# Two transformer blocks on one core: softmax scaling taken from the probabilities and put on the attention output

## What is computed

```python
# first block: kinds "a" (top-k selected keys, biased) and "b" (latent attention)
logits = jnp.where(mask, logits, -jnp.inf)
p = jax.nn.softmax(logits, axis=-1)
y = jnp.einsum('bhts,bshd->bthd', p, v)

# second block: kind "A" (mixture of dilated windows) and three branches with gates
def masked_softmax(logits, mask):
    p = jnp.exp(logits - m)
    den = jnp.sum(p, axis=-1, keepdims=True)
    return p / jnp.maximum(den, 1e-30)
gate = jax.nn.sigmoid(gl)
o_b = gate[..., 0:1] * o_cmp + gate[..., 1:2] * o_slc + gate[..., 2:3] * o_win
```

## Time and profile before

| | |
|---|---|
| median of 3 runs | 2970.11 us (2968.42 to 2970.17) |
| the profiled execution's own time | 2971.57 us |
| its span | 2969.6 us |
| busy PE / DVE / ACT / POOL | 88% / 50% / 22% / 68% |
| attention of block one, two layers | 338 to 454 and 1382 to 1499 us |
| attention of block two | 2335 to 2513 us |

### The profile page before, as it was taken

How to read it: one execution, slowest core, us unless ns; L and a number is a source line. 1 busy time by engine, 2 the same in 40 slices (tenths; PEclk the granted TensorE clock), 3 DMA queues, 4 the chain that set the end, 5 groups by cost and what they waited for, 6 DMA issues and landing times. The chain is left out here.

```text
span 2969.6 us, 35964 instructions
## 1 busy us (share of the span) xinstructions
PE 2617.5 (88%) x11363; PEld 1905.5 (64%) x11363; DVE 1480.9 (50%) x2231; ACT 647.6 (22%) x1406; POOL 2017.7 (68%) x988
## 2 busy tenths in 40 slices
PE   6876788989999988857889889999889888899998
PEld 3652456767777756524567667777587655677776
DVE  4789644336715437896353367244520243443243
ACT  1312451013201113124520123011100365110001
POOL 4562467877878865624568778788668744688886
PEclk9996888999999989977889999999869888899999
DMA  5130001222322222300012222222443100233232
GB/s 152 57 100 22 22 1 59 90 78 78 92 85 86 91 72 64 100 22 22 1 56 89 83 71 92 85 92 85 113 128 122 49 1 8 65 95 96 92 92 78
DMA packets 62115, 214.33 MB, mean 72 GB/s; under 512 B 6384, under 2 KB 6512, under 8 KB 61984
## 3 DMA queue, kind: packets, MB, share of 16 engines
q1 hardware_dynamic: 54144, 195.06, 21.2%
q10 hardware_dynamic: 7840, 17.58, 2.2%
HBM read 210.45 MB, written 10.01 MB: 74 GB/s over the span
## 5 line engine op out<-in xcount | busy, mean ns | idle before, releaser
L398 PE MATMUL out_tile<-arena_r,w_hi 128*128 128x512 f32 (+1 forms) x5474 | 1760.1, 403 | 0.0
L1388 POOL TENSOR_TENSOR w_hi<-weight_ring,cst 128x1024 fp32r<-128x1024 f32 x363 | 891.1, 2455 | 713.1 <-issue 508.5
L398 PE MATMUL out_tile<-arena_r,w_lo 128*128 128x512 f32 (+1 forms) x2737 | 1144.7, 418 | 126.5 <-DVE arena_r L1050 67.0
L398 PEld LDWEIGHTS out_tile<-arena_r,w_hi 128*128 128x128 f32 (+1 forms) x5474 | 1058.0, 194 | 249.7 <-issue 9.9
L1392 POOL TENSOR_TENSOR w_lo<-weight_ring,w_hi 128x1024 fp32r<-128x1024 f32 x363 | 903.4, 2489 | 28.4
L398 PEld LDWEIGHTS out_tile<-arena_r,w_lo 128*128 128x128 f32 (+1 forms) x2737 | 528.6, 193 | 372.3 <-issue 94.8
L1407 POOL TENSOR_SCALAR work<-work,small 128x128 f32<-128x128 f32 (+3 forms) x160 | 171.3, 1086 | 117.9 <-DVE small L1071 117.7
L1023 DVE TENSOR_TENSOR x<-out_tile,x 128x512 f32<-128x512 f32 x72 | 49.8, 692 | 388.8 <-PE out_tile L398 388.8
L826 ACT ACTIVATE work<-work,small 128x384 f32<-128x384 f32 (+4 forms) x256 | 134.2, 524 | 257.9 <-DVE small L1063 257.9
L991 DVE CAST arena_r<-work 128x512 f32 (+2 forms) x94 | 176.0, 1872 | 14.3 <-issue 12.7
L481 PE MATMUL turned<-cst,work 128*128 128x128 f32 (+1 forms) x592 | 125.8, 336 | 55.5 <-POOL work L1407 48.8
(11 more groups left out here) (131 smaller groups left out, 1972.1 us busy)
## 6 DMA issues: line engine op xcount, KB each, us to landing
weight_ring<-stream SPq DMA_DIRECT2D x364, 512.0 KB, 3.5
bias_rows<-bias_kept ACTq DMA_DIRECT2D x3, 2556.0 KB, 20.5
strips<-bias_rows ACTq DMA_DIRECT2D x3, 2048.0 KB, 9.7
x<-x_t SPq DMA_DIRECT2D x4, 512.0 KB, 8.5
arena<-bias_rows ACTq DMA_DIRECT2D x1, 2048.0 KB, 9.4
out_t<-arena SPq DMA_DIRECT2D x8, 256.0 KB, 2.2
cst<-consts ACTq DMA_DIRECT2D x1, 785.0 KB, 9.5
p<-par ACTq DMA_DIRECT2D x1, 221.0 KB, 11.0
```

The source lines that it names most:

```text
L398: ins = pe.matmul(out, l, r, start=start and n == 0, stop=stop and n == 2, **kw)
L1388: pool.tensor_tensor(w_hi[:, s % SPLIT, :].rearrange("p (w c) -> p w c", c=P), ring[:, s, :].rearrange("p (w c) -> p w c", c=P), ones.unsq ...
```

## The change

1. **No normalising of probabilities.** POOL's `normalise` and its semaphore go. The transposes wait for `exp_done` alone, so what is turned and multiplied by V are the bare exponentials.
2. **Reciprocals by group.** The row sums of a group's 8 items lie side by side (16 slots); DVE takes one reciprocal over 8 columns at the group's end, with the 1e-30 and, in block two, the gates on it.
3. **A scale bank per group.** After a group's last PV, PE waits for that reciprocal and makes 8 matmuls (L529): the stationary operand is one column of `rinv` repeated 64 times, the moving one the identity. The result is a 128x512 bank with each query's scale in its column, for both heads. It is put into the next of the two `turned` banks, and ACT copies it to SBUF (`scales`, L878).
4. **Scaling the PV bank.** DVE multiplies the `stat` bank by it (`finish1`, `finish2`), one iteration later than it split the bank before (`LAG_CLOSE` 4). Block one then splits the product. In block two cmp, sel and win now close on their own: 16 groups, not 8; DVE adds the three scaled results up and splits after win (and after A).
5. **ACT goes by pairs**: both exps of pair i, then both copies of pair i-2, then the scale bank where one is due.
6. After attention PE waits for `y_ready`, 8 splits.

```diff
-                                pe.wait_ge(sec.prob_ready, L * sec.turns + n + 1)
+                                pe.wait_ge(sec.exp_done, L * len(items) + n + 1)
+                                out = turn_bank(sec.item_turn[n])
...
+                            if closes(pair[0]):
+                                pe.wait_ge(sec.inverse_ready, L * sec.groups + group + 1)
+                                out = turn_bank(sec.scale_turn[group])
+                                for n in range(PER_GROUP):
+                                    at = group % 2 * PER_GROUP + n
+                                    ins = pe.matmul(out[n % 2 * HD:n % 2 * HD + HD, n // 2 * P:(n // 2 + 1) * P],
+                                                    rinv[:, at:at + 1].to_broadcast([P, HD]), ident,
+                                                    start=True, stop=True)
+                                ins.then_inc(sec.turn_done, 1)
...
+                for i in range(sec.pairs + LAG_PV):
+                    if i < sec.pairs:
+                        for n in (2 * i, 2 * i + 1):
...
+                            act.activation(work[:, n % 6, 0:w], work[:, n % 6, 0:w], ACT.Exp, scale=-1.0,
+                                           bias=negmax[:, n % 8:n % 8 + 1], accum_out=rsum[:, n % 16:n % 16 + 1])\
...
+                    if LAG_TURN <= i < sec.pairs + LAG_TURN:
+                        m = i - LAG_TURN
...
+                        for n in (2 * m, 2 * m + 1):
...
+                            act.wait_ge(sec.turn_done, L * sec.turns + t + 1)
...
+                    if i >= LAG_PV and closes(items[2 * (i - LAG_PV)]):
...
+                        act.activation(scales[:, group % 2, :], turn[t % 2][:, :], ACT.Copy).then_inc(sec.turn_taken, 1)
...
+                def finish1(kind, c, ps, g, signal):
+                    dve.tensor_tensor(y_one[:, 0, :], ps[:, :], scale1[:, g, :], ALU.mult).then_inc(signal, 1)
+                    dve.drain()
+                    split(y_one[:, 0, :], (y_a if kind == "a" else y_b)(c)).then_inc(y_ready, 1)
...
+            def finish2(kind, c, ps, g, signal):
+                total = (y_sum if kind == "cmp" else y_two)[:, 0, :]
+                dve.tensor_tensor(total, ps[:, :], scale2[:, g, :], ALU.mult).then_inc(signal, 1)
+                dve.drain()
+                if kind in ("sel", "win"):
+                    dst = y_sum[:, 0, :] if kind == "sel" else total
+                    dve.tensor_tensor(dst, y_sum[:, 0, :], total, ALU.add)
+                    dve.drain()
+                if kind in ("A", "win"):
+                    split(total, y_2(c + (0 if kind == "A" else 4))).then_inc(y_ready, 1)
...
-                part = work[:, n % 6, 0:NCMP if kind == "cmp" else (b + 1) * P]
-                pool.tensor_scalar(part, part, rinv[:, n % 8:n % 8 + 1], gate, ALU.mult,
-                                   ALU.bypass if gate is None else ALU.mult).then_inc(sec.prob_ready, 1)
```

More of the change, by code:

```diff
@@ L145, in opens, with turn_numbers @@
 def opens(item):
-    return item[2] == 0 and item[0] not in ("sel", "win")
+    return item[2] == 0
 def closes(item):
-    return item[2] == QB - 1 and item[0] not in ("cmp", "sel")
+    return item[2] == QB - 1
+def turn_numbers(items):
+    item_at, scale_at, count = {}, {}, 0
+    for i in range(len(items) // 2 + LAG_PV):
+        if LAG_TURN <= i < len(items) // 2 + LAG_TURN:
+            for n in (2 * (i - LAG_TURN), 2 * (i - LAG_TURN) + 1):
+                item_at[n] = count
+                count += 1
+        if i >= LAG_PV and closes(items[2 * (i - LAG_PV)]):
+            scale_at[2 * (i - LAG_PV) // PER_GROUP] = count
+            count += 1
+    return item_at, scale_at, count
 def attention_tiles(items):
@@ L191, in __init__ @@
         self.applied = len([k for k, _ in norms if k not in WIDE])
-        self.turns = len(items)
         self.pairs = len(items) // 2
-        self.groups = len([0 for n in range(self.pairs) if closes(items[2 * n])])
+        self.groups = len(items) // PER_GROUP
+        self.item_turn, self.scale_turn, self.turns = turn_numbers(items)
         self.tile_done = sem(name + "tile_done")
@@ L817, in take, with attention @@
                 act.activation(dst, psum[sec.tile_no(key) % 4][0:rows, :], ACT.Copy).then_inc(sec.taken["a"], 1)
-            def attention(sec, L, turned, width):
+            def attention(sec, L, turned, scales, width):
                 items = sec.items
[L822 to L837, removed]
@@ new lines, in attention @@
+                for i in range(sec.pairs + LAG_PV):
+                    if i < sec.pairs:
+                        for n in (2 * i, 2 * i + 1):
+                            sec.wait_taken(act, L, ("score",) + items[n])
+                            w = width(items[n])
+                            act.activation(work[:, n % 6, 0:w], work[:, n % 6, 0:w], ACT.Exp, scale=-1.0,
+                                           bias=negmax[:, n % 8:n % 8 + 1], accum_out=rsum[:, n % 16:n % 16 + 1])\
+                               .then_inc(sec.exp_done, 1)
+                    if LAG_TURN <= i < sec.pairs + LAG_TURN:
+                        m = i - LAG_TURN
+                        if m >= SLOTS:
+                            act.wait_ge(sec.pv_done, L * sec.pairs + m - SLOTS + 1)
+                        for n in (2 * m, 2 * m + 1):
+                            kind, h, b = items[n]
+                            t = sec.item_turn[n]
+                            act.wait_ge(sec.turn_done, L * sec.turns + t + 1)
+                            rows, w = (NCMP, P) if kind == "cmp" else (P, (b + 1) * P)
+                            act.activation(turned[0:rows, n % (2 * SLOTS), 0:w], turn[t % 2][0:rows, 0:w], ACT.Copy)\
+                               .then_inc(sec.turn_taken, 1)
+                    if i >= LAG_PV and closes(items[2 * (i - LAG_PV)]):
+                        group = 2 * (i - LAG_PV) // PER_GROUP
+                        t = sec.scale_turn[group]
+                        if group >= 2:
+                            act.wait_ge(sec.pv_taken, L * sec.groups + group - 1)
+                        act.wait_ge(sec.turn_done, L * sec.turns + t + 1)
+                        act.activation(scales[:, group % 2, :], turn[t % 2][:, :], ACT.Copy).then_inc(sec.turn_taken, 1)
@@ L1050, in norm_input, with attention @@
                         dve.tensor_tensor(lo, work[:, (k - 1) % 3, :], hi.bitcast(F32), ALU.subtract).then_inc(h_ready, 1)
-            def attention(sec, L, bias, width, target):
-                items, group = sec.items, 0
-                for i in range(sec.pairs + LAG_PV):
+            def attention(sec, L, bias, width, gate, finish):
+                items = sec.items
+                for i in range(sec.pairs + LAG_CLOSE):
                     if i < sec.pairs:
@@ L1064, in attention @@
                                                           ALU.add, ALU.min, negmax[:, c:c + 1]), sec)
-                    if 1 <= i <= sec.pairs:
-                        c, (kind, _, b) = 2 * (i - 1) % 8, items[2 * (i - 1)]
+                    if 1 <= i <= sec.pairs and closes(items[2 * (i - 1)]):
+                        group = 2 * (i - 1) // PER_GROUP
+                        kind, h, _ = items[2 * (i - 1)]
+                        sums, inverse = (s[:, group % 2 * PER_GROUP:(group % 2 + 1) * PER_GROUP] for s in (rsum, rinv))
@@ L1077, in attention @@
                         ins.then_inc(sec.inverse_ready, 1)
[L1078 to L1080 removed]
+                    if i >= LAG_CLOSE and closes(items[2 * (i - LAG_CLOSE)]):
+                        m = i - LAG_CLOSE
+                        group, (kind, h, _) = 2 * m // PER_GROUP, items[2 * m]
                         dve.wait_ge(sec.pv_done, L * sec.pairs + m + 1)
[L1082 to L1083 removed]
+                        dve.wait_ge(sec.turn_taken, L * sec.turns + sec.scale_turn[group] + 1)
+                        plain(dve)
+                        finish(kind, h // 2, stat[group % 2], group % 2, sec.pv_taken)
@@ L1438, in _ @@
             first, last = LAYERS * W1_TILES, LAYERS * W1_TILES + W2_TILES - W2_BLOCKS["pad"] // WT
[L1439 to L1457, removed]
+            with pool.Fori(first // RING, last // RING) as i:
                 group(i * RING, i)
```

72 lines of the change are left out of this document (40 added, 32 removed).

## The result

The changed kernel takes 2979.02 us (median of 8 runs, 2974.33 to 2984.25), the kernel before 2970.14 us beside it: a ratio of 1.0032, 95% interval [1.0021, 1.0043]. That is 9 us slower, inside the range and on the forecast's side. The profiled execution took 2984.25 us, its span is 2982.1 us, 12.5 us more than the span before; this execution lies 5 us above the median of the eight.

A forecast was written before the change was run, and what follows sets the result against it. PE was taken as attention's nearest bound, stalled by POOL and partly at the low clock. Terms of -13.4 us at full clock and +27 for clock falls made +14 on 2971.6: 2985 us, range 2950 to 3012.

The forecast's parts named there:

- POOL's stall goes, ACT's copies take its place: PE's transposes and scale matmuls in attention: waits for POOL vanish, waits for ACT's copies replace them, 1 to 2.5 us a group.
- the walk: One attention cycle stepped through PE, DVE and ACT with timeline durations: 12.75 us for kind b, 13.4 for kind a.
- the end: Last group's 512-key scores to output projection: 12.7 us, so -1.7 us in block one and +0.9 in block two.
- Block one at full clock: Block one's attention: 91.4 us for 99.6 and end -1.7, so -9.9 us per layer, -19.8 for two layers.
- The clock in block one: PE's clock in block one's attentions: falls in 5 of 8 a and 1 of 8 b cycles, 1.6 us each.
- a mean clock of 0.95 or more: Sign against the forecast: the mean granted clock in attention moving to 0.95 or more.
- Block two: Block two's attention: +6.4 us at full clock, plus falls in 2 of 3 A and 9 of 12 other cycles, 1.6 us each.
- the passage from the last A scores to the first of win: Block two's attention, between kind A and the first win: +0.4 us at full clock.
- Kind A: Block two's kind A cycles: 12.9 us each where three took 40.38; -2.1 us in the sum.
- The sum: Whole kernel: -13.4 us at full clock plus 27 for clock falls, +14 on 2971.6, giving 2985 us.
- Scale matmuls: PE in attention: 8 added per group, 1.02 us at full clock, 33 us for 32 groups; upper bound twice that.
- The rival of a PE bound: Attention: copies come sooner than walked, stalls and clock falls go against 33 us of scale matmuls: -59, 2913 us; chance 0.10.

The follow-up runs named there:

- e1: The changed kernel with ACT going item by item again (exp, copy, exp, copy, then the scale bank): 2955.03 us, ratio 0.9947 to the kernel before.
- e2: The changed kernel with ACT making both copies of pair i-2 before both exps of pair i: 2891.95 us, ratio 0.9735 to the kernel before.
- e3: The kernel before with only ACT's order by pairs (exp, exp, copy, copy), POOL's products left in: 2970.96 us, ratio 1.0001.
- g1: The kernel before with ACT making both copies of pair i-2 before both exps of pair i, POOL's products left in: 2969.76 us, ratio 0.9998.
- g2: The changed kernel with block two's 128-key scores of kinds A, sel and win computed four times instead of once: 2970.43 us, ratio 1.0006 to the kernel before.

## Why the prediction was right

- **POOL's stall goes, ACT's copies take its place**: shown by the waits, and by e1, e2, e3 and g1. This was the term that decided, and in kind b the walk held to a tenth: PE's wait before the 384-key transposes ends at 4.14 us of the cycle (414.96 less 410.82; walked 4.1), and a b cycle is 12.65 (12.75). The seven cycles of block one's first attention take 92.2 us (91.4; 343.99 to 436.15 in the timeline), the end 12.47 (12.7; to 448.62). The first of them missed most, 14.5 us for 12.9: the granted clock was 0.50 from the start of this attention to 346.
- **Block one at full clock, -19.8 us**: measured -19.8, as -9.0 and -10.7 for twice -9.9. That the sum agrees to the tenth is chance.
- **The clock in block one**: wrong. I took it to fall in 5 of 8 a cycles and 1 of 8 b cycles, +9.6 us. Behind the first pairs it fell in none, though kind a stalls 1.39 us in one piece. The term is 0. I had written that a mean clock of 0.95 or more would prove me wrong: for block one, at 0.96 and 0.97, it does.
- **Block two**: +6.4 at full clock and 11 falls at 1.6 us, +24.0 in all; measured +28.1. In the trace the clock fell around every cmp, in two of four sel and three of four win cycles, the 9 of 12 that I took, but also in all three A cycles, where I took 2, and once behind the last A scores (0.51 from 2364 to 2371), which I hadn't counted: 13 in all. A round was walked at 33.1, or 36.7 with its share of the falls, and took 37.2. The largest miss is the passage from the last A scores to the first of win: 38.3 us (2360.27 to 2398.53) for 32.3 before, +6.0 where my +0.4 and two falls make +3.6. The clock is low for 10.5 us there around sel (0.52 from 2378 to 2388.5), since scale matmuls and 512-key scores run slow one behind the other. The end took 14.64 (2510.28 to 2524.92; walked 12.7): the clock had fallen there too.
- **Kind A**: the sum had -2.1 for it, but three cycles at 12.9 for 40.38 are -1.7. The walk was too long as well: with the clock at 1.00, in g2, a cycle takes 12.3. With a fall in each it took 13.7, where the terms make 14.5. These errors hide each other.
- **The sum**: +13.8 forecast, +12.5 by the spans, +9 by the medians. That it came so near is partly luck: -9.6 (no falls in block one), +4.1 (block two) and +4.1 outside the attentions, which I had at nothing. Of the last, 2.6 us come behind block two's attention. There the projection's first matmul waits 3.88 us for DVE's closing where it waited 1.81, and then runs at a granted clock of 0.50 and 0.72 for its first 4 us where it had 1.00; from its start to DVE's taking of its first tile it is 7.3 us for 5.9. No run tells where the other 2.7 us come from.
- **Scale matmuls**: 1.02 us a group where the clock is full; 38.4 us busy in all. The DVE closing of 1.95 us took 1.9, its high part 0.43 for 0.4.
- **The rival of a PE bound** (2913, chance 0.10) was the right picture of another kernel: with the copies first it came to 2892. Its price fell short in both blocks: its terms make -38 us in block one's attentions and -21 in block two's, and they came to -51 and -31.

## What to carry to other kernels

When a slow stage between two engines is taken out, look for the next resource that the same instruction waits for, here a PSUM bank, and at the program order of the engine that frees it: a copy that frees a bank goes ahead of work that has slack. Walk one steady cycle with durations from the timeline, each engine in its own order; it gave the two stalls of kind b to a tenth of a microsecond before the kernel ran, and those of kinds a and A to 0.3. The walk doesn't give the clock: in block one that term alone was off by 9.6 us. Order and change were worth nothing or less apart and 78 us together, so an edit that comes out a little slower is worth one look at what the time now hangs on.

## What the runs showed of the hardware that I had not expected

More work made the kernel faster: 72 matmuls put into PE's wait took 8.6 us off the median, with the mean granted clock of block two's attention at 0.88 for 0.84. And the clock stayed up in block one behind stalls like those behind which it fell in block two: stalls of 1.39 us before the transposes and 0.98 us before the scale matmuls, in every cycle of kind a, with the granted clock at 1.00, while in kind A, with 1.50 and 0.90 us and the same score, transpose and PV matmuls, but without kind a's mask matmuls (0.73 us at 512 keys), it fell. The window of the changed kernel over the cycles of kinds a and b behind the first pairs:

```profile
349.00:436.00 87.00, 75.11 (x646) 51.57 (x646) 35.77 (x131) 54.45 (x172) 0.00 (x0) 1.00 0.01 2
```

Whether the mask matmuls decide wasn't tried. Nor does the length of one stall decide alone: behind the same 1.58 us after win's scores the clock held once (2402.53) and fell once (2439.10). The Trainium skill, "TensorE: Matmul & The Clock Gate", section "A second HAM failure mode: psum-queue depth-cycling", has, in a bf16 kernel that cycles through PSUM banks, short idle gaps between groups of matmuls take the clock again and again. Block two's rows agree with it (0.84), the row above doesn't; by that rule for every cycle, at the forecast's price of a fall, the kernel would have come to 3008 us, and it took 2979.
